# Eight multiplications of the recurrence's keys and receptances go from VectorE to GpSimd

## The reference

```python
w = -softplus(-(w0 + tanh(wd) @ w2)) - 0.5
decay = exp(-exp(w))
a = sigmoid(a0 + ad @ a2)
kk = (k * k_k) / norm(k * k_k)          # per head of 64
k = k * (1 + (a - 1) * k_a)
for t in range(512):                    # state: 64 x 64 for each of 8 heads
    sa = state @ -kk[t]
    state = state * decay[t] + outer(sa, kk[t] * a[t]) + outer(v[t], k[t])
    y[t] = state @ r[t]
bonus = sum(r * k * r_k) * v
```

## Time and profile before

| what | value |
|---|---|
| median of three runs | 2424.88 us |
| profiled execution, whole | 2425.5 us |
| its span | 2423.7 us |
| TensorE busy | 2334.2 us, 96% |
| VectorE busy | 1383.4 us, 57% |
| ScalarE busy | 981.0 us, 40% |
| GpSimd busy | 240.2 us, 10% |
| second attention kind, first layer | about 189 to 235 us |
| second attention kind, second layer | about 927 to 971 us |

### The profile page before, as it was taken

How to read it: one execution, slowest core, us unless ns; L and a number is a source line. 1 busy time by engine, 2 the same in 40 slices (tenths; PEclk the granted TensorE clock), 3 DMA queues, 4 the chain that set the end, 5 groups by cost and what they waited for, 6 DMA issues and landing times.

```text
span 2423.7 us, 35763 instructions
## 1 busy us (share of the span) xinstructions
PE 2334.2 (96%) x13448; PEld 1873.0 (77%) x13448; DVE 1383.4 (57%) x1936; ACT 981.0 (40%) x1507; POOL 240.2 (10%) x192
## 2 busy tenths in 40 slices
PE   8998999999999998999999999999999999999998
PEld 6775767888887775777888887777888888788887
DVE  4567767666545457767656546675443446543443
ACT  5545435323235545535323234564232233422332
POOL 0041210000022031311000012101000001000001
PEclk9999999999999999999999998999999999999999
DMA  4220014555432220014565421222332222232222
GB/s 159 78 76 12 20 54 145 193 193 193 144 104 78 87 70 27 19 37 140 192 196 192 157 98 59 87 83 93 99 100 95 95 95 70 79 99 98 97 95 87
DMA packets 68796, 248.33 MB, mean 102 GB/s; under 512 B 7632, under 2 KB 8144, under 8 KB 68688
## 3 DMA queue, kind: packets, MB, share of 16 engines
q1 hardware_dynamic: 68688, 246.85, 30.7%
HBM read 244.72 MB, written 2.10 MB: 102 GB/s over the span
## 4 chain that ended last, share of the span: by engine, by line
PE 84%; DVE 8%; ACT 5%; issue 3%; POOL 0%; DMA 0%; DVEq 0%; ACTq 0%; SPq 0%; POOLq 0%
PE dense L590 24%; PE dense L592 24%; PE dense L591 24%; PE aux L697 1%; ACT wh L1385 1%; DVE wl L2006 1%; PE aux L880 1%; PE aux L993 1%; PE aux L1004 1%; PE aux L1089 1%; PE dense L618 1%; DVE nt L2065 0%; ACT xh L1439 0%; PE aux L890 0%; PE aux L704 0%
## 5 line engine op out<-in xcount | busy, mean ns | idle before, releaser
L590 PE MATMUL dense<-xh,wh 128*128 128x512 f32 x1840 | 733.0, 398 | 27.9 <-DVE wl L2006 10.7
L1385 ACT ACTIVATE wh<-raw 128x1024 fp32r<-128x1024 f32 x346 | 366.7, 1060 | 962.5 <-PE dense L592 955.5
L592 PE MATMUL dense<-xh,wl 128*128 128x512 f32 x1840 | 718.7, 391 | 0.0
L591 PE MATMUL dense<-xl,wh 128*128 128x512 f32 x1840 | 718.6, 391 | 0.0
L2006 DVE TENSOR_TENSOR wl<-raw,wh 128x1024 fp32r<-128x1024 f32 x346 | 427.5, 1236 | 495.0 <-ACT wh L1385 493.4
L590 PEld LDWEIGHTS dense<-xh,wh 128*128 128x128 f32 x1840 | 347.0, 189 | 121.9 <-issue 23.1
L591 PEld LDWEIGHTS dense<-xl,wh 128*128 128x128 f32 x1840 | 346.9, 189 | 73.8 <-issue 4.3
L592 PEld LDWEIGHTS dense<-xh,wl 128*128 128x128 f32 x1840 | 346.7, 188 | 73.3
L590 PE MATMUL dense<-hidh,wh 128*128 128x512 f32 x928 | 363.6, 392 | 4.9 <-DVE hidl L2038 2.1
L591 PE MATMUL dense<-hidl,wh 128*128 128x512 f32 x928 | 361.9, 390 | 0.0
L592 PE MATMUL dense<-hidh,wl 128*128 128x512 f32 x928 | 361.8, 390 | 0.0
(11 more groups left out here) (393 smaller groups left out, 2404.2 us busy)
## 6 DMA issues: line engine op xcount, KB each, us to landing
raw<-stream SPq DMA_DIRECT2D x362, 512.0 KB, 3.4
mraw<-mod_stream SPq DMA_DIRECT2D x96, 512.0 KB, 4.3
x<-x_t SPq DMA_DIRECT2D x4, 512.0 KB, 6.8
y_t<-x SPq DMA_DIRECT2D x8, 256.0 KB, 2.0
cst<-consts SPq DMA_DIRECT2D x1, 993.0 KB, 9.2
band<-bands SPq DMA_DIRECT2D x1, 576.0 KB, 4.4
cond<-c_rows SPq DMA_DIRECT2D x1, 512.0 KB, 10.1
pv_next<-vecs SPq DMA_DIRECT2D x3, 82.5 KB, 4.4
```

Source lines behind the costliest of these rows:

```text
L590: pe.matmul(o, a, h, start=first, stop=False)
L591: pe.matmul(o, a, l, start=False, stop=False)
L592: return pe.matmul(o, b, h, start=False, stop=last)
L1385: act.activation(wh[:, slot].rearrange("p k m -> p (k m)"), raw[:, slot, :], ACT.Copy).then_inc(hi_done, 1)
```

## The change

The table `HATS` loses its "k" and "r" steps, and VectorE's code for them goes. GpSimd gets a function `decayed` that multiplies one tile by its exponential, eight calls per layer: four for keys, four for receptances. They stand between and behind GpSimd's key squares and bonus inputs of tiles 2 and 3. Each waits for its tile's exponentials and for the bonus input that still needs the unscaled tile. A new semaphore `kr_hats` counts them, and TensorE waits for all eight of a layer at the head of `prepare_chunks`.

```diff
-        HATS = {18: "a0", 19: "a1", 20: "a2", 21: "a3 k0", 22: "k1 n0", 23: "n1 b0", 24: "b1 k2",
-                25: "k3 s0", 26: "n2 s1", 27: "n3 b2", 28: "b3 s2", 29: "s3 r0", 30: "r1 r2",
-                31: "r3"}
+        HATS = {18: "a0", 19: "a1", 20: "a2", 21: "a3", 22: "n0", 23: "n1 b0", 24: "b1",
+                25: "s0", 26: "n2 s1", 27: "n3 b2", 28: "b3 s2", 29: "s3"}
...
                 pe.wait_ge(hats_ready, L + 1)
+                pe.wait_ge(kr_hats, L * 8 + 8)
...
-                    if step == "k":
-                        dve.wait_ge(exp_tile, k0 + p + 1)
-                        dve.wait_ge(rkk_ready, k0 + p + 1)
-                        tt(krv[:, 4 + p, :], krv[:, 4 + p, :], cum[:, p, :], MUL)
...
-                    if step == "r":
-                        dve.wait_ge(rkk_ready, k0 + p + 1)
-                        tt(krv[:, p, :], krv[:, p, :], e1[:, p, :], MUL)
...
-                for n in range(2):
-                    for p in (2 * n, 2 * n + 1):
-                        key_square(p)
-                    for p in (2 * n, 2 * n + 1):
-                        bonus_in(p)
+                def decayed(t, by, p):
+
+                    wait_apart(pool, exp_tile, L * 4 + p + 1)
+                    wait_apart(pool, rkk_ready, L * 4 + p + 1)
+                    pool.tensor_tensor(t, t, by[:, p, :], ALU.mult).then_inc(kr_hats, 1)
+
+                for p in range(2):
+                    key_square(p)
+                for p in range(2):
+                    bonus_in(p)
+                for p in range(2, 4):
+                    key_square(p)
+                decayed(krv[:, 4, :], cum, 0)
+                bonus_in(2)
+                decayed(krv[:, 5, :], cum, 1)
+                decayed(krv[:, 0, :], e1, 0)
+                bonus_in(3)
+                decayed(krv[:, 1, :], e1, 1)
+                for p in range(2, 4):
+                    decayed(krv[:, 4 + p, :], cum, p)
+                    decayed(krv[:, p, :], e1, p)
```

More of the change, by code:

```diff
@@ L434, in build @@
         mixh_ready, mixl_ready = sem("mixh_ready"), sem("mixl_ready")
+        kr_hats = sem("kr_hats")
         wag_ready, lh_ready, ll_ready = sem("wag_ready"), sem("lora_h"), sem("lora_l")
```

## The result

Eleven runs of the changed kernel have a median of 2431.97 us (2428.61 to 2435.35), eleven of the kernel before on the same chip 2427.44 us (2423.84 to 2429.65). The ratio is 1.002, with a 95% interval of 1.001 to 1.0029: slower, by 4.5 us (2.4 to 7.0). The forecast was 2427.7 us, +2.8 us on the three first runs, with "no change" as the likeliest case at 0.63. The time lies at the upper edge of the range (2421.5 to 2432), and the kernel moved to the slower side, to which I had given 0.26. Of the 4.3 us between forecast and median, 2.6 are in the base: eleven runs of before have their median that much above the first three.

The account below looks back on a forecast made before the run. TensorE bounds the whole span, VectorE is full in the stretch. Per layer 4.85 us more holds, less 4.2 removed, plus 0.38 and 0.37 of waits gave +1.4; two layers, +2.8 on 2424.88, gave 2427.7 us, range 2421.5 to 2432.

Parts of the forecast that it names:

- What bounds the stretch: Second attention kind, 935 to 965 us: VectorE is full, busy 29.24 of 30 us, and TensorE's transposes wait for it.
- What is removed: Eight VectorE instructions per layer at 0.60 us each, 4.8 us of VectorE per layer.
- The holds: VectorE instructions held behind GpSimd multiplications: ten per layer, 6.66 us in place of 1.81, so 4.85 us more.
- GpSimd's scaling by one column doesn't hold VectorE: Scaling L2848: VectorE's "a" takes its plain 0.68 us inside it, so no hold was counted.
- One layer's replay, times two: Queues of units 16 to 31 replayed with the second layer's pitches: +1.4 us per layer, two layers +2.8 us.
- give-back: End of the stretch, where the receptances stood: some of the +2.8 us at unit 24 comes back, leaving +1.4 per layer.
- Rival C: TensorE's clock in the attention: a half-clock dip costs 1.6 us; 2429.3 or 2426.1 us; chance within the forecast's 0.58.
- The sum: Two layers at +1.4 us give +2.8 us, on a base of 2424.88 us: 2427.7 us.
- Rival B: Weights of units 18 to 24: full loss at each hold, +3.5 us per layer, 2431.9 us; chance 0.25.
- Rival A: GpSimd's new multiplications run free beside VectorE: -2.0 us per layer, 2420.8 us; chance 0.15.
- Rival D: GpSimd late for TensorE's new wait at L993, for which it would have to lose 17 us; chance 0.02.

Follow-up runs that it names:

- kernel 11: The changed kernel again, unchanged, on another chip, timed and profiled a second time; median 2431.07 us, ratio 1.0013 to before.
- kernel 6: The kernel before with six unused matmuls per layer in TensorE's gaps at units 26 and 27; median 2427.47 us, ratio 1.0001 to before.
- kernel 7: The changed kernel with six unused matmuls per layer in TensorE's gaps at units 26 and 27; median 2430.04 us, ratio 1.0013 to before.
- kernel 1: The changed kernel without the eight key and receptance multiplications per layer on either engine; median 2420.9 us, ratio 0.9973 to before.
- kernel 2: The changed kernel with GpSimd's eight instructions scaling by a column instead of the exponentials' tile; median 2429.45 us, ratio 1.0005 to before.
- kernel 3: The changed kernel with only the four key multiplications on GpSimd, receptances back on VectorE; median 2428.69 us, ratio 1.0007 to before.
- kernel 4: The changed kernel with only the four receptance multiplications on GpSimd, keys back on VectorE; median 2433.36 us, ratio 1.0021 to before.
- kernel 5: The kernel before with only VectorE's table reordered, receptances and shifted products last, nothing on GpSimd; median 2428.53 us, ratio 1.0005 to before.
- kernel 9: The kernel before with VectorE's receptances and shifted products last, plus two unused matmuls per layer at units 26 and 27; median 2422.99 us, ratio 0.9979.
- kernel 10: The kernel before with two unused matmuls per layer in TensorE's gaps at units 26 and 27; median 2423.58 us, ratio 0.9984 to before.

## Why the prediction was wrong, step by step

**What bounds the stretch: right.** VectorE sets the pace of units 18 to 25, and transposes wait for its weights: The waits of the second layer's stretch (930 to 974 us after, 930 to 971 before; us in total, times, longest) of after:

```profile
PE aux L880 <- DVE wts L2226: 9.5, 9, 3.2
```

and of before:

```profile
PE aux L880 <- DVE wts L2225: 5.2, 8, 1.3
```

The 3.2 us in the first row are unit 16's transposes, which wait as long before, at 927.64, ahead of this window. Without them TensorE waits 6.3 us for the weights against 5.2: 2.4 us more up to unit 24, 1.3 less behind it.

**What is removed: right.** 16 tiles at 0.60 us pitch, less what was already beside TensorE.

**The holds: right in place, number and sum** (6.53 us measured, 6.66 forecast), and so were unit 24 (+2.70, forecast +2.8) and unit 31 (+1.27, forecast +1.4) in the second layer. A holder that has waited itself is longer on the page (1.71 in place of 1.27 us), as forecast.

**"GpSimd's scaling by one column doesn't hold VectorE": wrong.** It does, for its first half microsecond, and the sum had this hold at nothing. At the earlier trace rows "a" started 0.76 us into the scaling and took its plain 0.68; in the first layer after, it starts 0.15 us into it. GpSimd first, then VectorE:

```profile
201.10 1.56 POOL L2842 TENSOR_SCALAR rkb<-hats,pv 128x512 f32<-128x512 f32 x1 [2.64 <-PE dense L934]
```

```profile
201.25 1.08 DVE L2235 TENSOR_TENSOR bl<-bl 128x512 f32<-128x512 f32 x1
```

It ends at 202.33, 1.23 us behind the scaling's start; in the second layer 942.24 is 1.23 us behind 941.01 too. Less its own 0.68 us the hold lasts 0.55 us of GpSimd's 1.56; why it ends there no run shows. This costs the first layer 0.4 us. The Trainium skill (SBUF — State Buffer, section "Who interferes with whom") has the lock held for a whole instruction, by which "a" would have ended past 202.66. The trace disagrees for this form: "a" ended at 202.33.

**"One layer's replay, times two": the step that failed first.** The replay's +1.4 has a give-back at the end, where the receptances stood. It needs a TensorE that waits for VectorE. In the second layer, at full clock, units 27 to 31 take 7.89 us after and 8.86 before, 0.97 given back. In the first layer TensorE is at half clock from 225 to 232 us and is itself the bound: 10.15 against 10.42, only 0.27. Take 0.7 less given back and 0.4 more held, and +1.4 becomes the +2.5 measured. Where the first layer has no half clock (kernel 11) the give-back is whole, and the hold of 0.4 alone is left over: +2.0 in the table against +1.5 in the second layer. I had seen the half clock, but used it only as a price of 1.6 us for a spell more or less, not as a state in which the same change has another price.

**Rival C, the clock: too small a place.** I looked for it in the attention alone, and gave it no chance of its own. It added 1.9 us at 1100 us and 1.0 at 1485 in the first profile, 2.0 and 0.9 in the second; of these only the one at 1100 stays when the second profile of before is the base. Why it falls there is open: TensorE's work in front is the same in kernels that have the spell and in the one that has not.

**The sum.** Holds and gains in the stretch cost +3.5 us where the clock is level (1.5 and 2.0 in the table; +2.5, give or take 1.7, between kernels 6 and 7), where the sum had 2.8. In the timed runs the medians differ by +4.5 in one comparison and +3.2 in the other; the 22 runs of the changed kernel lie 3.6 us above the 94 of before, give or take 0.9. More half clock isn't what these runs have: their mean granted clock is 0.9884 and 0.9890 in the two comparisons, that of the 94 runs of before 0.9882. Over those 94 runs 0.001 of clock goes with 1.1 us (correlation -0.74), so at equal clock the change would cost about 4.1 us, an estimate. The 2.9 us at 1100 and 1485 us in the first profile are the difference of two executions, then, and not shown as a cost of the change; the profiled execution of before was one with little half clock (0.991). What the 0.7 us of lost give-back adds on the average isn't known either, since only two executions of each kernel were profiled. Of the 4.3 us between forecast and median, 2.6 are the base and 0.7 the stretch at level clock. The last 1.0 is no more than the runs leave open.

**Rival B** named the right side and, by luck, the right time (2431.9 against 2431.97), but its mechanism, full loss at every hold, is refuted by the 6.53 us. **Rivals A and D** are refuted by kernel 1 and by the 17 us to spare. Kernel 1's median of 2420.9 us is the 2420.8 that rival A would have given, in part by luck: the replay's -2.0 us per layer was about right (-2.1 and -2.2), but the base was 2.6 us too low, and a spell of 1.6 us was gone. With the forecast at +2.8 against a limit of 4.85, and holds that I knew I had bounded loosely, 0.26 for slower was too little.

## What to carry to other kernels

An elementwise tile of this size moved from a full VectorE to an idle GpSimd spares VectorE its 0.60 us and then holds a VectorE instruction that reads two SBUF tensors, or scales the weights, by up to 1.07 us here; list what VectorE has queued at that very time before counting idle GpSimd time as free, and prefer the column form where there is a choice, which holds for less (0.55 us). When a replay rests on a bound, look at TensorE's granted clock of every place where it is used: at the 1.2 GHz level 0.7 of 1.4 us of gain on VectorE vanished, because TensorE was the bound. Before a difference of two profiles is put down to the clock, compare the granted clocks of the timed runs. And where TensorE has gaps at the end of a stretch that waits for VectorE, two matmuls of no use, placed in the gaps, gained 3.8 us, where the reordering alone gained nothing, and six in the same places, on the old order, nothing either.

## What the runs showed of the hardware that was not expected

- GpSimd's 128x512 scaling by a column holds a VectorE two-tensor instruction for its first 0.55 us of 1.56.
- The same 22.4 us of work (TensorE busy 21.53 us in both) was followed by 6.8 us at a granted clock of 0.50 in two executions of the changed kernel and by none in two of before. Each kernel's runs spread over 4 to 13 us, and over the 94 timed runs of before the time falls as the mean granted clock rises (correlation -0.74, 1.1 us for 0.001).
- TensorE has an idle around 1050 us that the trace puts down to nothing: none in the two profiles each of before and of the changed kernel, nor in those of kernels 2 and 3, 0.4 to 1.0 us in those of kernels 1, 4, 5, 9 and 10, and 1.3 to 2.0 us in the three that have six small matmuls added in each layer, some 90 us earlier in this one.
